# A decoder layer with expert retrieval: dots ahead of selections on VectorE, query steps in another order and three chunks later, a norm's squares in PSUM

## The reference, cut to what matters

```python
x = x + gt1 * rmsnorm(y, g_post_mix[layer])          # y: output of the token mixer
h = rmsnorm(x, g_pre_ffn[layer]) * (1.0 + sc2) + sh2
y = peer_ffn(h, ...)
x = x + gt2 * rmsnorm(y, g_post_ffn[layer])

# peer_ffn
q = (hf @ w_q).reshape(T, PEER_HEADS, 2, PEER_DQ // 2)      # 16 query tiles of 128 columns
s = einsum('thcd,hckd->thck', q, sub_keys)                  # 16 x 128 scores a token
s1, i1 = top_k(s[:, :, 0], 16); s2, i2 = top_k(s[:, :, 1], 16)
cand = s1[..., :, None] + s2[..., None, :]                  # 256 candidates a head
top_s, pos = top_k(cand, 16)                                # expert_idx from pos, i1, i2
weights = softmax(top_s)
act = gelu(einsum('cd,ced->ce', hc, u[ec]))                 # a dot of 1024 with each expert's u
coef = act * wc
out = einsum('ce,ced->cd', coef, v[ec])                     # sum of the experts' v rows
```

## Time and profile before

| | us |
|---|---|
| median of three runs | 1040.91 |
| profiled execution | 1039.99 |
| its span | 1038.2 |

### The profile page before, as it was taken

One profiled execution on the slowest core, in us unless ns is written; L12 is line 12 of the kernel. 1 busy time (PEld: TensorE's weight loads), 2 busy tenths in 40 slices (PEclk: granted clock), 3 DMA queues, 4 the chain that ended last, 5 costly groups with the idle time before them and its releaser, 6 DMA issues.

```text
span 1038.2 us, 11466 instructions
## 1 busy us (share of the span) xinstructions
PE 923.9 (89%) x3505; PEld 558.9 (54%) x3505; DVE 732.7 (71%) x1937; ACT 293.9 (28%) x812; POOL 338.7 (33%) x329
## 2 busy tenths in 40 slices
PE   8999999999999999999999878868687786877787
PEld 6888888887646675556565333323233332333332
DVE  6699799664574277966867766866777677667455
ACT  4211122255474123322332221212312212212222
POOL 0101002011000044444534754545444544435440
PEclk9999999999999999999999988998898999889899
DMA  9976947897205769999999999999999999999994
GB/s 368 403 269 195 372 154 281 326 345 144 67 17 194 293 260 421 405 394 421 421 421 421 420 422 421 421 421 421 421 422 421 421 421 422 421 421 420 421 422 191
DMA packets 63436, 361.94 MB, mean 349 GB/s; under 512 B 7516, under 2 KB 8172, under 8 KB 30606
## 3 DMA queue, kind: packets, MB, share of 16 engines
q0 software_dynamic: 43424, 292.59, 69.3%
q1 hardware_dynamic: 19950, 68.61, 17.9%
HBM read 359.58 MB, written 1.59 MB: 348 GB/s over the span
## 4 chain that ended last, share of the span: by engine, by line
PE 57%; DMA 32%; DVE 6%; ACT 3%; issue 1%; POOL 1%; ACTq 0%; DVEq 0%; POOLq 0%
PE pb L596 20%; DMA arena<-in_peer_uv,idx 18%; PE pb L857 18%; DMA ring<-in_peer_uv,idx 11%; PE pb L614 3%; DMA hT<-in_peer_uv,idx 3%; PE pb L832 3%; PE pb L766 2%; PE pb L713 2%; PE pb L886 2%; PE pb L776 2%; DVE arena L1559 1%; PE pb L631 1%; PE pb L736 1%; ACT sig L1143 1%
## 5 line engine op out<-in xcount | busy, mean ns | idle before, releaser
L857 PE MATMUL pb<-arena,sig 128*128 128x512 f32 x412 | 199.4, 637 | 29.1 <-ACT sig L1143 29.1
L596 PE MATMUL pb<-hT,ring 128*128 128x256 f32 x752 | 162.8, 379 | 0.5 <-ACT arena L962 0.5
L553 POOL DMA_INDIRECT arena<-in_peer_uv,idx x102 | 119.3, 1169 | 120.6 <-PE pb L857 93.6
L857 PEld LDWEIGHTS pb<-arena,sig 128*128 128x128 f32 x412 | 82.9, 204 | 138.9 <-issue 138.2
L857 PE MATMUL pb<-ring,sig 128*128 128x512 f32 x288 | 134.5, 611 | 23.4 <-ACT sig L1143 23.4
L1559 DVE CUSTOM_DVE_ANT_0 arena<-arena,sig 128x1024 f32<-128x1024 f32 x104 | 124.3, 1224 | 42.8 <-DMA arena<-in_peer_uv,idx 42.3
L596 PEld LDWEIGHTS pb<-hT,ring 128*128 128x128 f32 x752 | 142.7, 190 | 21.1 <-ACT arena L962 1.7
L1140 ACT ACTIVATE gl<-dot 128x4 f32<-128x4 f32 (+1 forms) x73 | 15.0, 205 | 375.7 <-DVE dot L1559 375.5
L553 POOL DMA_INDIRECT ring<-in_peer_uv,idx x72 | 86.5, 1201 | 82.3 <-PE pb L857 71.9
L1559 DVE CUSTOM_DVE_ANT_0 ring<-ring,sig 128x1024 f32<-128x1024 f32 x72 | 87.3, 1224 | 32.6 <-DMA ring<-in_peer_uv,idx 32.1
L857 PEld LDWEIGHTS pb<-ring,sig 128*128 128x128 f32 x288 | 55.8, 198 | 98.1 <-issue 97.9
(11 more groups left out here) (327 smaller groups left out, 1228.7 us busy)
## 6 DMA issues: line engine op xcount, KB each, us to landing
ring<-in_w_stream SPq DMA_DIRECT2D x79, 512.0 KB, 7.2
arena<-in_w_ada POOLq DMA_DIRECT2D x32, 512.0 KB, 11.3
arena<-in_w_ada SPq DMA_DIRECT2D x12, 512.0 KB, 11.5
arena<-in_w_stream SPq DMA_DIRECT2D x8, 512.0 KB, 8.0
arena<-in_w1k SPq DMA_DIRECT2D x6, 512.0 KB, 7.9
more<-in_w_stream SPq DMA_DIRECT2D x6, 512.0 KB, 13.1
sig<-in_w_ada SPq DMA_DIRECT2D x4, 512.0 KB, 15.0
more<-in_w1v POOLq DMA_DIRECT2D x1, 2048.0 KB, 20.7
```

What stands on the lines that cost most here:

```text
L553: nc.gpsimd.indirect_dma_start(out=rowat[PLACE[n]][:, 0:2 * D if apart(n) < 0 else D], out_offset=None, in_=a["peer_uv"] if apart(n) < 0 e ...
L596: last = mm(pb[:, bank, 0:SEQ], w[:, k * P:(k + 1) * P], src[:, k, :], start=(k == 0), stop=(k == DT - 1))
L857: last = mm(pb[:, 4 + 2 * t + hf, :], diag[:, c % DEEP, e, :], rowat[PLACE[n]][:, D + hf * 512:D + (hf + 1) * 512], start=(i == 0 and e == ...
```

## The change

VectorE takes the dots of rows 4 to 7 ahead of parts 1 and 2 of unit 1's selection, and those of rows 8 to 11 ahead of the norms. The norms of tile 1 are cut in two (`out_norm`, `ffn_norm`) with part 0 of unit 2's selection between them; the selections of units from 3 on come two chunks later, and in the order parts 0, 1, 2 behind chunks 4k - 5, 4k - 4 and 4k - 3. TensorE does chunk 2 ahead of the transposes of tile 1, and the query steps from 6 on follow three chunks later; in each group of four the two full steps come first, those of tile 1 alone second. ScalarE follows both orders. Its squares for the second norm of tile 1 go into the PSUM banks of the mixer's output instead of y. `LATE` becomes 92.

```diff
-SOON, SLOTS, LATE = 12, 16, 84
+SOON, SLOTS, LATE = 12, 16, 92
@@
 for _m in (0, 2, 4):
-    STEPS += [(_m, (1,)), (_m + 1, (1,)), (_m + 6, (0, 1)), (_m + 7, (0, 1))]
+    STEPS += [(_m + 6, (0, 1)), (_m + 7, (0, 1)), (_m, (1,)), (_m + 1, (1,))]
 STEPS += [(m, (0, 1)) for m in range(12, 2 * PH)]
+AHEAD, STEP_AT = 6, 3
+def step_at(c):
+    i = AHEAD + c - STEP_AT
+    return i if AHEAD <= i < len(STEPS) else None
@@ TensorE
             subkey_scores(5)
+            expert_chunk(2)
             h2_transposes(1)
-            pe.wait_ge(a_h2T, DT // 2 + 2)
-            query_columns(6)
-            for c in range(2, TT * CPT):
+            for c in range(3, TT * CPT):
                 expert_chunk(c)
-                if c == 2:
-                    subkey_scores(6)
-                    query_columns(7)
-                if c + 5 < len(STEPS):
-                    subkey_scores(c + 5)
-                if c + 6 < len(STEPS):
-                    query_columns(c + 6)
+                if step_at(c - 1) is not None:
+                    subkey_scores(step_at(c - 1))
+                if c == STEP_AT:
+                    pe.wait_ge(a_h2T, DT // 2 + 2)
+                if step_at(c) is not None:
+                    query_columns(step_at(c))
@@ ScalarE
-                fn(squares[t], x[:, t, :], ACT.Square, accum_out=ss[:, 4 + t:5 + t]).then_inc(a_ss, 1)
+                fn(pb[:, OUT_BANK[t]:OUT_BANK[t] + 2, :].rearrange("p a b -> p (a b)"), x[:, t, :], ACT.Square,
+                   accum_out=ss[:, 4 + t:5 + t]).then_inc(a_ss, 1)
@@
             out_norm(1)
-            ffn_norm(1)
             gelu_next()
             query_out(5)
             score_out(4)
+            coefficients(2)
             score_out(5)
+            fn(turned[:, :], eps[:, :], ACT.Sqrt).then_inc(a_turn, 1)
+            ffn_norm(1)
+            unit_exp(1)
+            gelu_next()
             h2_out(1)
@@
-            query_out(6)
-            for c in range(2, TT * CPT):
+            for c in range(3, TT * CPT):
                 coefficients(c)
@@
-                if c + 4 < len(STEPS):
-                    score_out(c + 4)
-                if c + 5 < len(STEPS):
-                    query_out(c + 5)
+                if step_at(c - 2) is not None:
+                    score_out(step_at(c - 2))
+                if step_at(c - 1) is not None:
+                    query_out(step_at(c - 1))
@@ VectorE
             expert_dots(0)
-            for part in range(3):
-                retrieve(1, part)
+            retrieve(1, 0)
             expert_dots(1)
-            token_norms(1)
-            for c in range(2, TT * CPT):
+            retrieve(1, 1)
+            retrieve(1, 2)
+            expert_dots(2)
+            out_norm(1)
+            retrieve(2, 0)
+            ffn_norm(1)
+            for c in range(3, TT * CPT):
                 k, b = divmod(c, SEG)
                 expert_dots(c)
-                if c == 2:
-                    retrieve(2, 0)
-                if b and k + 2 < UNITS:
-                    retrieve(k + 2, b - 1)
+                if c == 3:
+                    retrieve(2, 1)
+                    retrieve(2, 2)
+                elif c > 6 and b != 2 and (c + 1) // SEG + 1 < UNITS:
+                    retrieve((c + 1) // SEG + 1, (c + 1) % SEG)
```

More of the change, by code:

```diff
@@ L1456, in first_h2, with out_norm @@
                 dve.wait_ge(v_h2, 3)
-            def token_norms(t):
+            def out_norm(t):
                 dve.wait_ge(a_ss, TT + 2 * t + 1)
@@ L1468, in token_norms, with ffn_norm @@
                 V_.tensor_tensor(scaled[t], x[:, t, :], rows[1], ALU.mult).then_inc(v_sc, 1)
+            def ffn_norm(t):
                 dve.wait_ge(v_sc, 2 * t + 2)
```

## The result

The changed kernel took 1042.76 us (median of 18 runs, 1040.96 to 1043.98) against 1040.62 us for the kernel before in the same jobs (18 runs, 1039.66 to 1041.46): a ratio of 1.0021, 95% interval 1.0014 to 1.0027, so 2.1 us slower (1.5 to 2.8). The forecast was 1042.0 in a range of 1038.8 to 1045.0.

What follows compares the result with a forecast made beforehand. The gather of expert rows at about 421 GB/s was taken as the bound, with a 2.73 us hole; holes of 2.05 + 1.8 = 3.85 us gave +1.1, so 1042.0 us for the median, range 1038.8 to 1045.0.

Steps and rivals of the forecast that it cites:

- VectorE's order up to row 16: VectorE around chunk 1: idle from 396.4 to 404.05, row 16's gather moves from 407.52 to 410.1, no loss.
- Chunk 2 ahead of the norms: On TensorE, chunk 2 starts at 415.7, 3.9 us earlier than before.
- Norms, and the square in PSUM: VectorE and ScalarE, tile 1's split norms: square priced -0.2 to +0.4 us, covered by a selection part, costed at nothing.
- Chunk 3: On TensorE, starts at 429.2, 3.7 us earlier, after idling from 424.4; the clock drop costs +1.9 us; chunk 4 at 441.4.
- Steps in another order, and SP's tiles: Query steps: chunks 5, 6, 7 at 452.2, 461.3, 470.2; SP's weight tiles sent later, removing 3.7 us of queue filling before 456.
- The ledger: DMA bytes done against row requests: 2.05 us lost at rows 24, 28, 32 plus 1.8 carried over, 3.85 against 2.73 before.
- LATE and the late selections: Ring limit 92 and selections two chunks later: cost nothing, gathers landing about 20 us after issue instead of 26.2.
- the case of the starved queue: Rival: late selections starve the DMA queue at each of 13 units, 16 us, 1057; chance 0.03.
- The sum: Whole kernel: holes of 3.85 against 2.73 us, so +1.1 us, giving 1042.0 for the median.
- is all that this change can win: DMA rate from 436 to 456: the hole there, 2.73 us, is the most the change could win back.
- the case in which the holes close: Rival: earlier slots, no clock drop and no thin queue return all 2.73 us, 1038.2; chance 0.12.
- The case of a draw: Rival: the same ledger at the full clock, +0.4 us, 1041.3; chance 0.10.

Runs made afterwards that it cites:

- the early copies: Changed kernel plus two 0.52 MB DRAM-to-DRAM copies on SP's queue, asked for once 9 and 11 rows are used: 1043.53 us, ratio 1.0025 to the kernel before.
- the filled idle time: Changed kernel plus five unread matmuls on TensorE between the transposes and chunk 3: 1041.40 us, ratio 1.0004 to the kernel before.
- without a stall: The stall: hole-free kernel (1039.69 us) plus a POOL wait holding row 200's gather until row 195 is used; 1044.59 us, ratio 1.0042 to the kernel before.
- interleaved: Changed kernel with each group's four query steps as full, single, full, single: 1041.13 us, ratio 1.0002 to the kernel before.
- the first experiment: Kernel before, step order kept: later query steps, chunks 3 and 4 dots before unit 2's selection, later selections from unit 3, LATE 92; 1039.69 us, ratio 0.9988.
- late copies: Changed kernel plus two 0.52 MB DRAM-to-DRAM copies once 101 and 103 rows are used, run twice: 1044.10 and 1045.76 us, ratios 1.0032 and 1.0050.
- dots ahead alone: Kernel before with only the dots of rows 4 to 7 ahead of parts 1 and 2 of unit 1's selection: 1044.36 us, ratio 1.0029.
- the 20 of ten: Changed kernel plus ten unread matmuls on TensorE between the transposes and chunk 3: 1043.86 us, ratio 1.0023 to the kernel before.

## Why the prediction was right or wrong

Step by step, the changed kernel's times less 1.31 us:

- *VectorE's order up to row 16: right.* Idle before the product for 7.04 us (some 7), row 16 at 410.15 (410.1), no hole there. The dots alone brought nothing, and the experiment with them alone showed more: without the rest of the change they cost 3.0 us, through a second idle time and a drop of the clock that my step did not have.
- *Chunk 2 ahead of the norms: right.* 415.69 (415.7).
- *Norms, and the square in PSUM: right, cost nothing.* The square took 1.01 us against 1.06, h2 was done at 423.3 (423.5).
- *Chunk 3: right in place, slightly high in price.* Idle 4.57 us (4.8), start 429.00 (429.2), length 8.40 us, so 1.5 us for the clock instead of 1.9. Chunk 4 at 440.86 (441.4).
- *Steps in another order, and SP's tiles: right.* Chunks 5, 6 and 7 at 451.6, 460.7 and 469.6 (452.2, 461.3, 470.2), tile 12 at 460.9 (461). That as many bytes at that place fill the queue is shown by the early copies.
- *The ledger: right as a count of holes.* Rows 24, 28 and 32 asked for at 432.69, 443.01 and 454.39, against 432.9, 443.55 and 454.35; holes of 3.9 us (3.85), so 1.1 to 1.2 more than before, as forecast. Of them 1.8 us were the part that the ledger did not explain before and that I carried over; no run measures it by itself. The Trainium skill, DMA: Bandwidth & Descriptors, section Measured, gives 6.15 us for 1 MB. My estimate from it was up to 3.7 us for each hole, 6.15 less the 2.49 of a row in the stream. The trace has 3.9 for all three, so the estimate disagrees with it again; the page's figure itself was not tested.
- *LATE and the late selections: right.* No effect, in an experiment of their own. 421 GB/s up to 1020, so the case of the starved queue is out.
- *The sum: +1.1 forecast, +1.5 in chunk 1 to end, +2.1 (1.5 to 2.8) in the runs.* The interval leaves out the forecast's 1.1. By the landing signals the middle of the last row comes 1.2 us later, which is the hole's part, and the last signal lies another 0.2 behind it, together the 1.5 of the profiles. The 0.6 between profiles and runs is not assigned.

What was wrong is the exchange rate behind the sum: a microsecond of hole as a microsecond of time. Closing 2.6 us of hole gave back 1.1; making one of 9.8 us cost 3.2 (5.6 by the runs); the filled idle time closed 0.6 of hole and brought 1.9. At the rate of the first of these, 1.1 us more of hole is worth 0.5 us, which falls short of the 1.5 and 2.1 measured. So that +1.1 came as near as it did is partly luck: the sum had no term for how far the last DMA engine is behind the others, and between these two kernels that distance happened to stay the same (7.1 and 7.3 us), where it ranges from 6.1 to 8.2 in the kernels without a stall. So the statement that 2.73 us "is all that this change can win", and with it the 1038.2 of the case in which the holes close, was too optimistic: with its hole all but closed, the best kernel got 1039.69. The case of a draw may be mis-sized the other way: it gave the full clock 0.7 us, the runs 1.8, with 0.6 as the lower end. And the order of the steps seems to cost more than the ledger had for it (interleaved, 2.0 us less in the runs, 0.8 to 3.2). Filled idle time and interleaved steps would together bring 3.8 us by the ratios, more than the 2.1 that the change lost; with such intervals the two may still add up, and they weren't run together.

So the events are the ones forecast, one by one: earlier chunks, an idle TensorE with its clock drop, a queue without its filling, and 1.1 us more of hole. The step from the hole to the time is the one that the runs do not bear out.

The best version found is the first experiment's, 1039.69 us.

## What to carry to other kernels

When a stream of transfers sets the time, keep a ledger of when each is asked for and when the queue before it is done, with every queue's bytes in it: loads that happen to stand in a thin stretch are worth as much there as earlier requests. But a dip in the mean rate of all DMA engines is not yet time lost; read the last microseconds of the stream too, since one engine's worth of work running alone there says that the others had time to spare. And when dots or norms are moved ahead on VectorE, look first for what ScalarE and then TensorE do meanwhile: the idle time in front of a chunk can be paid twice, as itself and as its first rows at the lower clock.

## What the runs showed of the hardware

- The DMA engines do not end together: with a mean of 421 GB/s up to the end, the stream of the changed kernel tails off through 60 and 26 GB/s (one engine's share) in 6 us. The sixteen landing signals of one row run apart along the stream, from 1.9 us at row 64 to 8.7 at row 255 in the kernel before, and a stall of 9.8 us brings them together again, from 7.6 to 0.3 us.
- After the same idle time of 4.57 us on TensorE, chunk 3 took 8.40 us in the changed kernel and 9.5 us in both kernels with late copies, with the same instructions around it; the first row took 3.41 and 3.75 us, and a row at 2.4 GHz takes 1.88. An idle time of 2.09 us was followed by the lower clock in the kernel with dots ahead alone (a step of 3.77 us instead of 1.95); in the first experiment's kernel two of 2.85 and 2.84 us, in front of 607.41 and 617.36, were not, and the granted clock is 1.00 from 600 to 629 there. So the length of one idle time does not tell whether the clock falls.
- A float32 product of 128x512 stands in the trace as two matmul records: the 10 records of five products took 4.46 us, the 20 of ten took 8.75, so 0.87 to 0.89 us a product.
